# Eight-column feature tiles of the samples turned by one transpose instead of eight, in three projections

## The reference

```python
h = rmsnorm(x, g_norm[l])
a_u, a_v, a_z, b_q, b_k, b_v, b_gd, b_z, c_q, c_z, gl = split_proj(h, w_in[l])
a_u, a_v = gelu(a_u), gelu(a_v)
vn = layernorm(a_v, ...)                        # A: per-head mixing over positions
out_a = a_u * (spatial_mix(vn, w_s, b_s)) * silu(a_z)
S = exp(g) * S + k[..., None] * v; o = q @ S    # B: gated linear attention, per sample one step
out_b = rmsnorm(o, gn_g) * silu(b_z)
p = softmax(q @ mk.T / 16); out_c = (p @ mv) * silu(c_z)   # C: attention into 256 memory rows
x = x + (sum_i sigmoid(gl_i + b_i) * (out_i @ w_branch_i)) @ w_out
```

## Time and profile before

| | |
|---|---|
| Median of 3 runs | 871.77 us (871.34 to 872.13) |
| Profiled execution, its own time | 871.54 us |
| Its span, first to last instruction | 869.8 us |
| Mean granted TensorE clock | 0.999 |
| TensorE (PE) busy | 854.6 us, 98% |
| VectorE (DVE) busy | 423.7 us, 49% |
| ScalarE (ACT) busy | 376.6 us, 43% |
| GpSimd (POOL) busy | 90.7 us, 10% |
| DMA traffic | 126.11 MB, 145 GB/s |

### The profile page before, as it was taken

How to read it: one execution, slowest core, us unless ns; L and a number is a source line. 1 busy time by engine, 2 the same in 40 slices (tenths; PEclk the granted TensorE clock), 3 DMA queues, 4 the chain that set the end, 5 groups by cost and what they waited for, 6 DMA issues and landing times.

```text
span 869.8 us, 16391 instructions
## 1 busy us (share of the span) xinstructions
PE 854.6 (98%) x6975; PEld 826.9 (95%) x6975; DVE 423.7 (49%) x737; ACT 376.6 (43%) x596; POOL 90.7 (10%) x129
## 2 busy tenths in 40 slices
PE   7999999999999999999999999999999999999997
PEld 6999999999999999999999999999989999999995
DVE  5524542634554466323346778645343544445634
ACT  7534445246665442322232256433234544534424
POOL 1001000000000222101012147000110000000000
PEclk9999999999999999999999999999999999999999
DMA  8325743231322669523466951425563332252402
GB/s 294 80 87 170 250 146 97 93 104 49 97 99 75 217 212 348 175 67 106 164 215 213 323 194 49 148 98 194 194 243 98 97 123 72 98 189 79 145 2 99
DMA packets 86068, 126.11 MB, mean 145 GB/s; under 512 B 3058, under 2 KB 72736, under 8 KB 86000
## 3 DMA queue, kind: packets, MB, share of 16 engines
q1 hardware_dynamic: 72288, 76.58, 27.1%
q0 software_dynamic: 13616, 48.48, 15.7%
q10 hardware_dynamic: 96, 0.06, 0.0%
HBM read 112.91 MB, written 12.19 MB: 144 GB/s over the span
## 4 chain that ended last, share of the span: by engine, by line
PE 95%; DMA 1%; DVE 1%; ACT 1%; issue 1%; POOL 0%; ACTq 0%; DVEq 0%; POOLq 0%; SPq 0%
PE mm L1016 64%; PE mm L981 5%; PE mm L994 4%; PE mm L970 3%; PE mm L1303 2%; PE mm L1228 2%; DMA raw<-in_w_in_dram 1%; PE p L955 1%; PE p L957 1%; PE p L956 1%; PE mm L1249 1%; PE mm L1248 1%; PE mm L1247 1%; PE p L1155 1%; PE p L1185 1%; PE p L1129 1%
## 5 line engine op out<-in xcount | busy, mean ns | idle before, releaser
L1016 PE MATMUL mm<-h_lo,w_hi 128*128 128x260 f32 (+1 forms) x1088 | 223.3, 286 | 1.7 <-ACT tok L620 1.7
L1016 PE MATMUL mm<-h_hi,w_hi 128*128 128x260 f32 (+1 forms) x1088 | 219.0, 283 | 0.0
L1016 PE MATMUL mm<-h_hi,w_lo 128*128 128x260 f32 (+1 forms) x1088 | 218.5, 282 | 0.0
L1390 DVE TENSOR_TENSOR w_lo<-raw,w_hi 128x1024 fp32r<-128x1024 f32 x130 | 158.2, 1220 | 95.1 <-ACT w_hi L530 94.1
L1016 PEld LDWEIGHTS mm<-h_lo,w_hi 128*128 128x128 f32 x1088 | 167.9, 188 | 7.7 <-issue 6.0
L1016 PEld LDWEIGHTS mm<-h_hi,w_hi 128*128 128x128 f32 x1088 | 167.5, 188 | 0.0
L1016 PEld LDWEIGHTS mm<-h_hi,w_lo 128*128 128x128 f32 x1088 | 167.5, 188 | 0.0
L530 ACT ACTIVATE w_hi<-raw 128x1024 fp32r<-128x1024 f32 x130 | 135.9, 1053 | 7.5 <-issue 3.3
L1016 PE MATMUL mm<-x_lo,w_hi 128*128 128x260 f32 (+1 forms) x448 | 96.2, 284 | 0.0
L1016 PE MATMUL mm<-x_hi,w_hi 128*128 128x260 f32 (+1 forms) x448 | 95.3, 283 | 0.0
L1016 PE MATMUL mm<-x_hi,w_lo 128*128 128x260 f32 (+1 forms) x448 | 95.1, 282 | 0.0
(11 more groups left out here) (358 smaller groups left out, 1361.2 us busy)
## 6 DMA issues: line engine op xcount, KB each, us to landing
raw<-in_w_in_dram SPq DMA_DIRECT2D x44, 1024.0 KB, 5.3
raw<-in_w_branch_dram SPq DMA_DIRECT2D x12, 1024.0 KB, 5.1
raw<-in_w_mem_kv_dram SPq DMA_DIRECT2D x8, 1024.0 KB, 5.6
gate<-in_cache_mem_k_dram POOLq DMA_DIRECT2D x16, 512.0 KB, 6.0
tok<-in_cache_mem_v_dram POOLq DMA_DIRECT2D x14, 512.0 KB, 5.8
tok<-in_state_gla_dram POOLq DMA_DIRECT2D x8, 512.0 KB, 6.8
out_dram<-tok POOLq DMA_DIRECT2D x8, 512.0 KB, 6.4
work<-scr_q POOLq DMA_DIRECT2D x8, 512.0 KB, 4.9
```

Source lines behind the costliest of these rows:

```text
L1016: ins = MM(mm[:, j % 2, a, 0:c1 - c0], wp[:, j, k, :], xp[:, k, c0:c1], start=(k == 0 and wp is w_hi and xp is xl), stop=(k == KT - 1 and ...
L1390: V.tensor_tensor(w_lo[:, j], raw[:, j // 2, :, (j % 2) * P:(j % 2 + 1) * P], f32(w_hi[:, j]), ALU.subtract).then_inc(split_done, 1)
```

## The change

`stage` no longer holds the samples' columns of the halved blocks. ScalarE copies them, 8 columns a tile, to `qsT` (which it did for CQ only), 16 small copies more, and its two copies to `stage` are 8 columns shorter. One transpose (rows_turn) turns all of `qsT`, 128 partitions x 64, into 64 rows of 128: in the first tile of BZ, of PB and of AU. The row of sample `b` is then eight pieces of 128 values, on partitions `8k + b`. VectorE copies the 64 rows once (to `rows8`, a corner of `state`, or to `work`), POOL stores them to DRAM, and the eight pieces of a sample are brought together by the DMA that reads them back. For `a_v` this way through DRAM is new: POOL stores the rows to `scr_a`, waits, and loads `stok` from it, behind the loads for the layer norm and ahead of its own L467. New or other waits stand on `rows_T`, `dq_T`, `rows_up`, `vs_stored`, `as_stored` and `as_loaded`.

```diff
-    scr_v = nc.dram_tensor("scr_v", [B, D], F32, kind="Internal").ap()
-    scr_q = nc.dram_tensor("scr_q", [B, D], F32, kind="Internal").ap()
+    scr_v = nc.dram_tensor("scr_v", [KT * B, P], F32, kind="Internal").ap()
+    scr_q = nc.dram_tensor("scr_q", [KT * B, P], F32, kind="Internal").ap()
+    scr_a = nc.dram_tensor("scr_a", [KT * B, P], F32, kind="Internal").ap()
+        rows8 = state[0:KT * B, 0, 0:P]
@@ gpsimd
-            pool.wait_ge(tr_used, TR["BV"] + KT)
-            pool.dma_start(scr_v, stok[:, :]).then_inc(sem("vs_stored"), 16)
+            pool.wait_ge(sem("rows_up"), 1)
+            pool.dma_start(scr_v, rows8).then_inc(sem("vs_stored"), 16)
-                pool.dma_start(v_bc[b % 2], scr_v[b:b + 1, :].broadcast_to([P, D])).then_inc(sem(f"row_loaded{b % 2}"), 16)
+                row = scr_v.rearrange("(k b) c -> b k c", b=B)[b:b + 1].broadcast_to([P, KT, P])
+                pool.dma_start(v_bc[b % 2].rearrange("p (k c) -> p k c", c=P), row).then_inc(sem(f"row_loaded{b % 2}"), 16)
-            pool.dma_start(scr_q, work[0:B, 2048:2048 + D]).then_inc(sem("dq_stored"), 16)
+            pool.dma_start(scr_q, work[0:KT * B, 2048:2048 + P]).then_inc(sem("dq_stored"), 16)
...
             pool.dma_start(ws_raw, w_s[0].rearrange("h t s -> t h s")).then_inc(sem("ws_loaded"), 16)
+            pool.wait_ge(sem("rows_up"), 2)
+            pool.dma_start(scr_a, rows8).then_inc(sem("as_stored"), 16)
+            pool.wait_ge(sem("as_stored"), 16)
+            pool.dma_start(stok[:, :].rearrange("b (k c) -> b k c", c=P), scr_a.rearrange("(k b) c -> b k c", b=B)).then_inc(sem("as_loaded"), 16)
@@ scalar, evac_halves
-                A(stage[:, 0, 0:TT - 256], mm[:, 0, 0, 0:TT - 256], f)
-                A(stage[:, 1, 0:TT - 256], mm[:, 1, 0, 0:TT - 256], f).then_inc(evac_done, 1)
+                for u in range(2):
+                    A(qsT[:, 4 * it + j - 1 + u, :], mm[:, u, 0, 256:TT - 256], f)
+                A(stage[:, 0, 0:256], mm[:, 0, 0, 0:256], f)
+                A(stage[:, 1, 0:256], mm[:, 1, 0, 0:256], f).then_inc(evac_done, 1)
@@ tensor, to_tokens and hooks
-                if name in HALVED:
-                    ins = TRP(p67[0:B, j % 2, 0:P], stage[:, j % 2, 256:TT - 256], ident[:, :])
+            def rows_turn(bank):
+                return TRP(bank[0:KT * B, 0:P], qsT[:, :, :].rearrange("p k b -> p (k b)"), ident[:, :])
+                if name in BEHIND and c == 0:
+                    pe.wait_ge(evac_done, first(name))
+                    rows_turn(p67[:, 1, :]).then_inc(sem("rows_T"), 1)
                 if name == "PB" and c == 0:
                     pe.wait_ge(sem("qs_ready"), KT)
-                    for k in range(KT):
-                        ins = TRP(p67_8[0:B, k, :], qsT[:, k, :], ident[:, :])
-                    ins.then_inc(sem("dq_T"), 1)
+                    rows_turn(p67[:, 0, :]).then_inc(sem("dq_T"), 1)
@@ vector
-                        V.tensor_copy(stok[:, cs], p67[0:B, j % 2, 0:P]).then_inc(sem("stok_in"), 1)
+                if name in BEHIND and c == 1:
+                    dve.wait_ge(sem("rows_T"), BEHIND.index(name) + 1)
+                    if name == "AU":
+                        dve.wait_ge(sem("st_stored"), 16)
+                    V.tensor_copy(rows8, p67[0:KT * B, 1, 0:P]).then_inc(sem("rows_up"), 1)
-                    V.tensor_copy(work[0:B, 2048:2048 + D].rearrange("p (a b) -> p a b", a=2), p67[0:B, :, :]).then_inc(sem("dq_ready"), 1)
+                    V.tensor_copy(work[0:KT * B, 2048:2048 + P], p67[0:KT * B, 0, 0:P]).then_inc(sem("dq_ready"), 1)
-                        dve.wait_ge(sem("st_stored"), 16)
+                        dve.wait_ge(sem("as_stored"), 16)
@@ vector, gla_state(0) and layer_norm
+                    dve.wait_ge(sem("vs_stored"), 16)
-                    dve.wait_ge(sem("stok_in"), 2 * KT)
+                if n == NT:
+                    dve.wait_ge(sem("as_loaded"), 16)
...
```

More of the change, by code:

```diff
@@ L442, in load_q @@
             def load_q(b):
-                pool.dma_start(q_bc[:, b % 3], scr_q[b:b + 1, :].broadcast_to([P, D])).then_inc(sem(f"row_loaded{b % 3}"), 16)
+                row = scr_q.rearrange("(k b) c -> b k c", b=B)[b:b + 1].broadcast_to([P, KT, P])
+                pool.dma_start(q_bc[:, b % 3].rearrange("p (k c) -> p k c", c=P), row).then_inc(sem(f"row_loaded{b % 3}"), 16)
             for b in range(3):
@@ L644, in evac @@
                         act.wait_ge(tr_done, TR["BV"] + KT)
+                        act.wait_ge(sem("rows_T"), 1)
                     else:
@@ L892, in _ @@
                 if name == "AV":
+                    act.wait_ge(sem("dq_T"), 1)
                     act.wait_ge(stage_used, ST["PB"] + KT)
@@ L1161, in decode @@
                     pe.wait_ge(tr_used, TR["AV"] + KT)
-                    pe.wait_ge(sem("stok_in"), 2 * KT)
+                    pe.wait_ge(sem("rows_up"), 2)
                     for m in range(MT):
```

## The result

The changed kernel takes **896.02 us** (median of 4 runs, 894.77 to 897.41) against 871.94 for the kernel before in the same comparison: ratio 1.0277, 95% interval 1.0265 to 1.0290. It is 24 us slower where 2 us less was forecast. The profiled execution took 894.77, its span is 893.0, its mean granted clock 0.988.

A forecast was written before the change was run, and what follows sets the result against it. The prediction took TensorE, 95% of what ended last, to bound the kernel. Transposes at -2.29 us and the layer norm path at +0.3 made -2.0, so 871.77 became 869.8 us; range 868.9 to 872.2.

The forecast's parts named there:

- the row loads: 16 broadcasts read in 512-byte pieces, in GB and AV: +0.4 us issue, 0 to +1 us until landing, no cost in time.
- two estimates of slack: Room for later row loads: 1.4 us in GB before the row is needed, 1.3 us in AV behind the key tile.
- signs of being wrong: Mix wait above 3 us, DVE waiting for rows in AV or GB, rows landing over 2 us later, among others.
- Rival 3: Broadcasts in 512-byte pieces cost twice their DMA time, five rows inside AV overrun slack: +1.4 us, 873.2; chance 0.10.
- the packets of `w_s`: About 3.6 KB a packet on q0 during that load, taken as showing that small pieces are not sent one by one.
- The estimate by the Trainium skill's rule: About 3 cycles overhead a packet: 16% more DMA time a row, 0.24 us, below every slack named.
- The transposes: TensorE loses 24 and gains 3, 21 steps of 0.109 us: 2.29 us saved before the first mix.
- ScalarE and DVE: Copies added and removed in the pairs and AU's second tile: cost nothing; without cover 2.8 us.
- the second path: VectorE's layer norm, 508 to 545 us, delayed by POOL's later L467: +0.3 us, bounds +0.8 and -1.4.
- rival 1: POOL late in full before the mix, layer norm ends 0.8 to 1.4 us later: about 870.6 us; chance 0.20.

## Why the prediction was wrong

The step that failed is **the row loads: "Cost: nothing"**. It took the load of `w_s` as "exactly this form": 128 x 8 pieces of 512 bytes. The destination and the size of the pieces are the same, but `w_s` gives every partition pieces of its own, while a row load asks 128 times for the same eight, and these lay 4,096 bytes apart. The forecast allowed 1 us more until landing. Measured: 5.4 to 7.0 us more until landing for each of the 16 loads (medians), and about 2.5 us more of all DMA engines' time per load. Its two estimates of slack, 1.4 and 1.3 us, looked at the tile that the load brings and at the key tile behind it. In GB the first was simply overrun: VectorE waited up to 5.6 us for a row, which is one of the prediction's own signs of being wrong, and PE waited 4.6 us for VectorE's `tok`, where the prediction had said that "DVE's update is not what PE waits for there". In AV the transfer that hurt was another: SP's weights, on the same 16 engines, landed after 33 and 24 us instead of 9 to 12, and stopped PE for 15.1. The view of the earlier trace rows had shown that this stretch has 4% of DMA time free.

Rival 3 had the right place and the right reason in one clause, "8 small pieces that all partitions read", and held the packets of `w_s` against it. Packets do not tell: the kernel before with only the layout put in has 13,616, exactly as without, and is 24 us slower. Rival 3 decided from 1.2 us a row, and 2.5 was measured, more than its double price; its "three times the price would give over 880" was nearer than its 873.2. It let the excess fall on the wait at the first mix, where it was 0.7 us; it fell on the tiles behind AV and on GB.

The estimate by the Trainium skill's rule in "DMA: Bandwidth & Descriptors", section "Why small descriptors are slow (HBM only)" (16%, 0.24 us a row), was too small by ten at 4 KB. With the same pieces 1 KB apart q0's share is 16.6% of 869.0 us, 144.3 in all, 7.7 more than before, 0.5 a row (0.4 against the kernel with rows in one stretch, 15.9% of 869.3): of the rule's order, although nearly twice as much. What mattered is the distance of shared pieces, not their size.

**The transposes** were right. 2.29 us forecast, 2.37 measured. The new form takes 271 ns under way like the old, and its step in the chain is 0.11 us like the old one's:

```profile
L1047 PE MATMUL p<-ident,qsT x3: 271/271/272, 174.4 to 516.4; 128*64 128x128 f32 x3
```

```profile
516.55 0.11 PE p L1047
```

**ScalarE and DVE** were right. PE's waits for the halved blocks' last copy did not change (1.7 us in two, before and in every kernel with repaired loads), and the second path came earlier together with PE.

**The second path** was right in mechanism and off in size. "L467 starts near 515" is 511.92 + 2.94 = 514.9 in the time of before (543.29 - 540.35 = 2.94 apart at the mix), and "L1410 ends near 517.9" is 514.89 + 2.94 = 517.8. I took +0.3, between 0 and 0.7; 0.64 was measured, the late bound. What I had not priced is the clock behind that wait: with 2.14 us idle PE's clock fell, which cost another 1.0 for the 48 matmuls and 0.4 for the products. The sum from the rows is -2.37 + 0.64 + 1.4 = -0.3. The medians of 871.07 and 870.81 against 871.81 show -0.7 and -1.0; in the profiled executions the rest is the start, 0.34 and 0.57 us earlier. Whether the start is earlier for a reason in the change no run here settles: over the 13 profiles it lies between 27.85 and 29.09, early in the changed kernel (27.89), not early in the kernels with the early store (28.56) or with the queries' pieces only (28.49).

So without the pitch of 4,096 B the time would have been about 871, near rival 1 (870.6) and in part for its reason; with the store moved up, 869.4, 0.4 better than the forecast of 869.8. That nearness says nothing for the forecast of this kernel: it is a kernel with other loads and another place of the store.

## What to carry to other kernels

When a DMA's pattern changes, compare the addresses it reads, not only the size of its pieces: how many partitions ask for the same ones, and how far apart they are. If a tile has to be scattered, do it in the one small store, not in the large loads that read it many times; if it can't be, keep shared pieces off a pitch of 2 or 4 KB (half a KB more than 4 was enough here, and 1 KB cost no time). And the slack of a dearer transfer is that of everything that shares the engines, first the weights of the busiest engine, not only of what the transfer brings.

## What the runs showed of the hardware

- A load of 512 KB in which 128 partitions read the same eight pieces of 512 B took 11.9 us to land with the pieces 4,096 B apart, 8.2 at 2 KB, 6.7 at 1 KB, 5.0 in one stretch, 7.2 at 4,608 B; 6.0 where all 1,024 pieces were different and agreed in their place within 4 KB. Slow loads keep the DMA engines busy (0.81 to 0.95) at 77 to 137 GB/s.
- The clock behind a short wait. In 13 profiled kernels PE stood idle before the first mix for 1.46 to 1.55 us in four, and the products behind took 1.13 us at the higher level each time. In nine it stood idle for 2.12 to 2.29 us; in seven of them the products or the 48 matmuls behind ran partly at the lower level (6.82 to 7.96 us instead of 5.95), in two (those with the queries' loads replaced) they did not. So a wait that is 0.7 us longer cost 0.7 us in some executions and 2 in most; what decides between them stays open. One of the nine, of the kernel with the V rows' pieces only:

```profile
545.69 2.22 issue
547.90 1.13 PE p L1172 x8
549.19 7.48 PE mm L1030 x48
```

- A store of 32 KB issued behind four loads of 512 KB on the same queue landed 6.8 us after its issue, ahead of them 4.1. The size was the same; the other traffic of the stretch was not held equal.
